# Decode state in half batches through four buffers, and decode key scores with the transposes one step ahead

## The reference

```
def ssd_recurrent(xs, dt, a, bm, cm, h0):            # state update, one step
    h = h * exp(dt * a) + outer(x * dt, b)           # h: 8 x 32 heads x 64 x 128, f32: 1 MB a row
    y = einsum(c, h)                                 # contraction over the 128 states
    return y, h                                      # the new h is an output

def indexer_scores(iq, ik, iw):                      # 8 heads, dimension 64
    dots = relu(einsum('bthd,bsd->bths', iq, ik))    # ik: 4096 cached keys per row, in pages of 128
    return einsum('bths,bth->bts', dots, iw * IDX_SCALE)
```

## Time and profile before

| | us |
|---|---|
| runs of the kernel before | 5871.83, 5881.72, 5880.62 |
| their median | 5880.62 |
| the profiled execution | 5866.49 |
| its span | 5864.7 |
| mix stage with the decode work, layer 0 | 759 to 1112 of the span |
| the same, layer 1 | 3185 to 3545 |

### The profile page before, as it was taken

The page is one execution under the profiler, slowest core; times in us unless marked ns, Lnnn a source line. Parts: engine busy times, 40 slices in busy tenths (PEclk is TensorE's granted clock), DMA queues, the critical chain, the costliest instruction groups (busy, mean ns, idle before and its releaser), DMA issues. The chain is left out here.

```text
span 5864.7 us, 54435 instructions
## 1 busy us (share of the span) xinstructions
PE 4418.7 (75%) x17752; PEld 2782.1 (47%) x17752; DVE 3518.7 (60%) x7869; ACT 1258.5 (21%) x3195; POOL 2478.8 (42%) x2215
## 2 busy tenths in 40 slices
PE   7948356777977798579778676968777677766988
PEld 5338245545444486253344565553334644642333
DVE  4061766596567632876676848966767467374334
ACT  2041132112133201120332311121232112111111
POOL 0000134334543322446565322456655345366776
PEclk9968567788988899889889888988888888888999
DMA  4316388667865585689889955689888977998999
GB/s 136 115 62 221 103 300 309 232 210 247 306 235 190 160 278 168 224 292 378 299 300 328 331 196 195 208 291 346 316 285 301 323 262 263 319 337 339 409 409 383
DMA packets 650608, 1555.20 MB, mean 265 GB/s; under 512 B 61416, under 2 KB 322120, under 8 KB 643816
## 3 DMA queue, kind: packets, MB, share of 16 engines
q0 software_dynamic: 307200, 1115.82, 53.1%
q1 hardware_dynamic: 330168, 401.65, 20.7%
q10 hardware_dynamic: 12960, 34.26, 1.5%
HBM read 1505.63 MB, written 45.93 MB: 265 GB/s over the span
## 5 line engine op out<-in xcount | busy, mean ns | idle before, releaser
L2749 PE MATMUL duo<-vring,diag 128*128 128x512 f32 (+1 forms) x3036 | 1549.3, 660 | 376.8 <-DMA vring<-in_peer_v,eidx 207.2
L2619 POOL DMA_INDIRECT uring<-in_peer_u,eidx x1024 | 1191.7, 1164 | 1373.0 <-DVE uring L2657 1034.5
L2702 POOL DMA_INDIRECT vring<-in_peer_v,eidx x1024 | 1122.2, 1096 | 1362.6 <-PE duo L2749 717.7
L2657 DVE SCALAR_TENSOR_TENSOR uring<-uring,xr 128x1024 f32<-128x1024 f32 x904 | 1091.8, 1221 | 259.2 <-DMA uring<-in_peer_u,eidx 221.9
L2749 PEld LDWEIGHTS duo<-vring,diag 128*128 128x128 f32 (+1 forms) x3036 | 601.8, 208 | 1160.0 <-issue 1010.2
L711 PE MATMUL duo<-wx,xT 128*128 128x512 f32 (+3 forms) x1440 | 605.7, 579 | 30.3 <-PEq L154 30.3
L2730 ACT ACTIVATE diag<-ident,wt 128x128 f32<-128x128 f32 x743 | 281.5, 397 | 823.2 <-PE duo L2749 708.3
L711 PEld LDWEIGHTS duo<-wx,xT 128*128 128x128 f32 (+1 forms) x1440 | 240.8, 179 | 382.5 <-issue 379.7
L2782 DVE SCALAR_TENSOR_TENSOR x_tok<-vring,wt,x_tok 128x1024 f32<-128x1024 f32 x281 | 365.0, 1299 | 65.4 <-DMA vring<-in_peer_v,eidx 39.3
L555 PE MATMUL duo<-xT,wx 128*128 128x264 f32 (+1 forms) x1536 | 356.7, 396 | 20.7 <-ACT newcols L578 17.8
L555 PEld LDWEIGHTS duo<-xT,wx 128*128 128x128 f32 x1536 | 302.0, 198 | 76.5 <-issue 25.1
(11 more groups left out here) (466 smaller groups left out, 5220.1 us busy)
## 6 DMA issues: line engine op xcount, KB each, us to landing
wx<-in_w_in SPq DMA_DIRECT2D x32, 2048.0 KB, 9.4
wx<-in_w_in SPq DMA_DIRECT2D x48, 1024.0 KB, 8.3
wm<-in_w_in SPq DMA_DIRECT2D x48, 1024.0 KB, 11.2
wm<-in_w_branch_a SPq DMA_DIRECT2D x48, 1024.0 KB, 10.6
wq<-in_peer_wq SPq DMA_DIRECT2D x48, 1024.0 KB, 9.7
wm<-in_w_branch_b SPq DMA_DIRECT2D x24, 1024.0 KB, 5.5
wm<-in_w_out SPq DMA_DIRECT2D x24, 1024.0 KB, 7.1
tokm<-tout ACTq DMA_DIRECT2D x64, 256.0 KB
```

The costliest lines, as they stand in the source:

```text
L2619: pool.indirect_dma_start(out=E.rings.urows[K % E.ur], out_offset=None, in_=table, in_offset=bass.IndirectOffsetOnAxis(ap=E.tiles[q][3][:, ...
L2657: dve.scalar_tensor_tensor(row, row, 1.0, xr, ALU.mult, ALU.mult, accum_out=G.pre[:, q % 2, j:j + 1]).then_inc(G.dotted, 1)
L2702: pool.indirect_dma_start(out=E.rings.vrows[K % E.vr], out_offset=None, in_=table, in_offset=bass.IndirectOffsetOnAxis(ap=E.tiles[q][3][:, ...
L2749: mm = pe.matmul(G.bank[6 + c][0:m, :], G.diag[:, R % DR, 0:m], E.rings.vrows[K % E.vr][:, c * BANK:(c + 1) * BANK], start=first, stop=las ...
```

## The change

It has three edits and one table.

State in half batches: `s_h` becomes four buffers of half a row (512 KB) in place of two of a whole one. Load, update and store go by halves i = 2b + hf, and buffer i % 4 is loaded again once half i is reduced and stored.

Outer halves: ACT's two halves of the outer product get places of their own, at b - 0.1 and b + 0.1 rows, where both stood at b + 0.1.

Scores one step ahead: transposes and copies of step e + 1 stand ahead of the dots, relu and reductions of step e, on TensorE, ACT and VectorE. The key gathers move one step earlier on GpSimd.

The table: ssm has 80 units instead of 130, scores 55 instead of 80, the mix stage covers 165 units instead of 240, and job S has 405 in all.

```diff
         self.gss, self.grs = self.sb("gss", [P, 1]), self.sb("grs", [P, 1])
-        self.h, self.u = self.sb("h", [P, 2, CPP, NST]), self.sb("u", [P, CPP, NST])
+        self.h, self.u = self.sb("h", [P, STATE_RING, CPP // 2, NST]), self.sb("u", [P, CPP, NST])
...
-KEYS_STEP, KEYS_RING, KV_RING = 16, 4, 4
+KEYS_STEP, KEYS_RING, KV_RING, STATE_RING = 16, 4, 4, 4
...
 HOT_ROWS = 4 * TOPK_S // PK
-SAMPLE_PARTS = (("ssm", 0.0, 130.0), ("qkv", 130.0, 30.0), ("scores", 160.0, 80.0), ("topk", 240.0, 130.0), ("attend", 378.0, 102.0))
-SAMPLE_TIME = 480.0
+SAMPLE_PARTS = (("ssm", 0.0, 80.0), ("qkv", 80.0, 30.0), ("scores", 110.0, 55.0), ("topk", 165.0, 130.0), ("attend", 303.0, 102.0))
+SAMPLE_TIME = 405.0
...
+def state_half(state, i):
...
+    half = CPP // 2 * NST
+    return state[i // 2].rearrange("h p n -> (h p n)").rearrange("(q x) -> q x", q=P)[:, i % 2 * half:(i % 2 + 1) * half]
...
     G, sem, at, n = J.G, J.sem, span(0), DECB
-    state = [G.state_ssm[J.l, b].rearrange("h p n -> (h p n)").rearrange("(q x) -> q x", q=P) for b in range(n)]
...
+    def load(i):
+        r = i % STATE_RING
+        sp.dma_start(J.h[:, r].rearrange("p c n -> p (c n)"), state_half(G.state_ssm[J.l], i)).then_inc(sem(f"hin{r}"), 16)
...
     sp.dma_start(J.dsk2[:], G.dsk[0:n, :]).then_inc(sem("skip"), 16)
-    for b in range(2):
-        sp.dma_start(J.h[:, b].rearrange("p c n -> p (c n)"), state[b]).then_inc(sem(f"hin{b}"), 16)
+    for i in range(STATE_RING):
+        load(i)
...
     for b in range(n):
+        for hf in range(2):
+            i = 2 * b + hf
+            if i + STATE_RING < 2 * n:
+                yield at(0.2 + 0.65 * (b + 0.8 + 0.2 * hf) / n)
+                sp.wait_ge(sem("reduced"), i + 1)
+                sp.wait_ge(sem(f"hout{i % STATE_RING}"), 16 * (i // STATE_RING + 1))
+                load(i + STATE_RING)
...
         sp.dma_start(J.ytf[CPP * b:CPP * (b + 1), :], J.yq[:, b, :]).then_inc(sem("yin"), 16)
-        if b + 2 < n:
-            sp.wait_ge(sem(f"hout{b % 2}"), 16 * (b // 2 + 1))
-            sp.dma_start(J.h[:, b % 2].rearrange("p c n -> p (c n)"), state[b + 2]).then_inc(sem(f"hin{b % 2}"), 16)
...
     act.activation(J.ztf[:], J.ztf[:], ACT.Silu).then_inc(sem("zs"), 1)
+    yield at(0.2)
+    act.wait_ge(sem("xdq"), 16 * n)
     for b in range(n):
-        yield at(0.2 + 0.65 * (b + 0.1) / n)
-        if b == 0:
-            act.wait_ge(sem("xdq"), 16 * n)
-        act.wait_ge(sem("bcast"), b + 1)
         for hf in range(2):
+            yield at(0.2 + 0.65 * max(0.0, b - 0.1 + 0.2 * hf) / n)
+            act.wait_ge(sem("bcast"), b + 1)
...
             last.then_inc(sem("outer"), 1)
-        yield at(0.2 + 0.65 * (b + 0.6) / n)
-        act.wait_ge(sem("stepped"), 2 * (b + 1))
-        act.dma_start(G.ssm_sample[J.l, b].rearrange("h p n -> (h p n)").rearrange("(q x) -> q x", q=P),
-                      J.h[:, b % 2].rearrange("p c n -> p (c n)")).then_inc(sem(f"hout{b % 2}"), 16)
+        for hf in range(2):
+            i = 2 * b + hf
+            r = i % STATE_RING
+            yield at(0.2 + 0.65 * (b + 0.4 + 0.15 * hf) / n)
+            act.wait_ge(sem("stepped"), i + 1)
+            act.dma_start(state_half(G.ssm_sample[J.l], i), J.h[:, r].rearrange("p c n -> p (c n)")).then_inc(sem(f"hout{r}"), 16)
...
     act.activation(J.grs[:], J.grs[:], ACT.Sqrt).then_inc(sem("groot"), 1)
-    act.wait_ge(sem("hout0"), 16 * n // 2)
-    act.wait_ge(sem("hout1"), 16 * n // 2)
+    for r in range(STATE_RING):
+        act.wait_ge(sem(f"hout{r}"), 16 * 2 * n // STATE_RING)
...
     for b in range(n):
-        hb = J.h[:, b % 2]
...
         for hf in range(2):
-            c = slice(half * hf, half * (hf + 1))
+            c, i = slice(half * hf, half * (hf + 1)), 2 * b + hf
+            hb = J.h[:, i % STATE_RING]
             yield at(0.2 + 0.65 * (b + 0.2 + 0.15 * hf) / n)
-            dve.wait_ge(sem("outer"), 2 * b + hf + 1)
-            if hf == 0:
-                dve.wait_ge(sem(f"hin{b % 2}"), 16 * (b // 2 + 1))
-            dve.scalar_tensor_tensor(hb[:, c], hb[:, c], J.eaq[:, b:b + 1], J.u[:, c], ALU.mult, ALU.add).then_inc(sem("stepped"), 1)
+            dve.wait_ge(sem("outer"), i + 1)
+            dve.wait_ge(sem(f"hin{i % STATE_RING}"), 16 * (i // STATE_RING + 1))
+            dve.scalar_tensor_tensor(hb, hb, J.eaq[:, b:b + 1], J.u[:, c], ALU.mult, ALU.add).then_inc(sem("stepped"), 1)
...
             dve.wait_ge(sem("stepped"), 2 * b + hf + 1)
-            own(dve.tensor_tensor(J.u[:, c], hb[:, c], cb, ALU.mult))
+            own(dve.tensor_tensor(J.u[:, c], J.h[:, (2 * b + hf) % STATE_RING], cb, ALU.mult))
...
         if e >= KEYS_RING:
-            yield at(0.1 + 0.88 * (e - KEYS_RING + 1) / (2 * NE))
+            yield at(0.1 + 0.88 * (e - KEYS_RING) / (2 * NE))
...
         dve.tensor_copy(J.skT[:, e % 2, BANK:], G.bank[4][:]).then_inc(sem("kT_d"), 1)
+    yield at(0.1 + 0.88 * 0.2 / (2 * NE))
+    copy(0)
     for e in range(2 * NE):
-        yield at(0.1 + 0.88 * (e + 0.2) / (2 * NE))
-        copy(e)
         yield at(0.1 + 0.88 * (e + 0.7) / (2 * NE))
+        if e + 1 < 2 * NE:
+            copy(e + 1)
...
     J.enter(act, 2)
-    for e in range(2 * NE):
-        yield at(0.1 + 0.88 * (e + 0.2) / (2 * NE))
...
+    def copy(e):
...
         act.activation(J.skT[:, e % 2, 0:BANK], G.bank[3][:], ACT.Copy).then_inc(sem("kT_a"), 1)
+    yield at(0.1 + 0.88 * 0.2 / (2 * NE))
+    copy(0)
+    for e in range(2 * NE):
         yield at(0.1 + 0.88 * (e + 0.6) / (2 * NE))
+        if e + 1 < 2 * NE:
+            copy(e + 1)
...
     J.enter(pe, 2)
-    for e in range(2 * NE):
-        yield at(0.1 + 0.88 * e / (2 * NE))
...
+    def turn(e):
...
                 tr.then_inc(sem("kturned"), 1)
+    yield at(0.1)
+    turn(0)
+    for e in range(2 * NE):
         yield at(0.1 + 0.88 * (e + 0.4) / (2 * NE))
+        if e + 1 < 2 * NE:
+            turn(e + 1)
...
 ORDER_SAMPLE = BACK + FRONT
-PLAN_SAMPLE = {"mix": 240, "norm2": 4, "pscore": 74, "route": 56, "norm1": 4, "xbc": 32, "tokproj": 70}
-PLAN_SAMPLE_SPLIT = {"mix_b": 240, "norm2_b": 4, "pscore_b": 50, "route_b": 80, "norm1": 4, "xbc": 32, "tokproj": 70}
+PLAN_SAMPLE = {"mix": 165, "norm2": 4, "pscore": 74, "route": 56, "norm1": 4, "xbc": 32, "tokproj": 70}
+PLAN_SAMPLE_SPLIT = {"mix_b": 165, "norm2_b": 4, "pscore_b": 50, "route_b": 80, "norm1": 4, "xbc": 32, "tokproj": 70}
...
```

## The result

| | before | changed kernel |
|---|---|---|
| median of the runs, us | 5876.64 (4 runs) | 5797.09 (4 runs, 5792.99 to 5802.14) |
| ratio, 95% interval | | 0.9865 [0.9848, 0.9882] |
| profiled execution: span, us | 5864.7 | 5792.5 |

The change takes 80 us off, 1.35%.

What follows compares the result with a forecast made beforehand. No engine bounds the whole; in the scores TensorE and VectorE wait for each other, and DMA and VectorE fill the loop. Scores -38, clock -6, loop -10, qkv +10: -44 us, 5822 profiled, 5837 as median; range 5798 to 5872.

Steps and rivals of the forecast that it cites:

- Waits of the scores: Key scores: TensorE's waits before the dots go when transposes run one step ahead; -19 us in each layer.
- Clock: Key scores: dots and transposes return partly to full TensorE clock; -4 us in layer 0, -2 in layer 1.
- State loop: State loop, per layer: less other work -6, 4 KB rows +4, fewer VectorE waits for state loads -3; sum -5 us.
- the term of moved work: State loop: 10.5% of the other 22.3 MB of DMA traffic leaves the loop; -6 us per layer.
- Half transfers: State loop: half batches cut rows from 8 to 4 KB and slow state transfers; +4 us per layer, bounds 0 to +7.
- Prelude and tail: Stretches before and after the state loop: chains of small transfers that fewer instructions beside them don't shorten; 0 us.
- qkv: Stretch before the key scores: takes 0.057 more of the stage's other work; +6 us in layer 0, +4 in layer 1.
- ACT by halves: State loop: outer products earlier in ACT's queue park it longer, taken in by TensorE's idle time; 0 us, bounds 0 to +20.
- B: Rival, chance 0.16: all 16 us of clock return, qkv +0, prelude and tail -14, loop 6 more; -84 us, 5797.
- C: Rival, chance 0.20: in the scores TensorE waits for VectorE's copies before the transposes instead, qkv +14; -15 us, 5866.
- D: Rival, chance 0.06: state halves arrive late in the saturated state loop, +48 us; in all +22 us, 5903.
- E: Rival, chance 0.08: mix stages are held elsewhere, the scores' gains fall to the stage's other chains; no change, 5880.

Runs made afterwards that it cites:

- fill: Kernel before with 8 extra identity transposes per scores step, placed where TensorE waits before the dots; ratio 0.9990 [0.9978, 1.0003].
- table_only: Kernel before with the new table alone (ssm 80, scores 55, mix stage 165 units); ratio 1.0019 [1.0008, 1.0029].
- no_table: Changed kernel with the old table (ssm 130, scores 80, mix stage 240 units); ratio to the kernel before 0.9884 [0.9868, 0.9901].
- state_only: Kernel before with the state in four half buffers and the outer halves placed apart, scores and table as before; ratio 1.0013 [0.9996, 1.003].

## Why the prediction was wrong

*Waits of the scores (-19 and -19).* Right in cause, and near in size. TensorE's idle time fell by 22.2 and 20.8 us, 5 us more than forecast; of it the forecast's leftover of 3 us shows as 5.1 and 1.8 us of waits for VectorE's copy.

*Clock (-4 and -2, bounds -10.2 and -5.9).* This term failed. TensorE's busy time fell by 14.4 and 16.3 us, 31 instead of 6, and that is 25 of the 36 us by which the forecast gain of 44 was short of the 80. Added up by line, 12.7 and 14.7 us of it are faster records, still beyond both bounds. I had priced full clock on two lines alone, dots and transposes, and left out the other lines that run between them, though the earlier trace rows gave the clock for the whole stretch: 0.83 over 96 us of busy time and 0.87 over 114. The two lines kept to their bounds, with 6.9 and 5.0 us. The others, put at nothing, gave 5.8 and 9.7 (L2226 alone 2.1 and 5.2). I then took less than half of a bound that was too small, with the reason that slow sets also follow other idle time. The fill run speaks against that discount: filling the waits before the dots, with the useful work in its old order, already brought 7 and 10 us. The Trainium skill (TensorE: Matmul & The Clock Gate, "Loop structure matters more than you think") puts it so that whether matmuls stay warm is decided by the loop nest. The trace of layer 1 agrees: with the same matmuls and fewer waits between them its clock went from 0.87 to 0.97.

*State loop (-5 and -5).* Layer 0 -3.3, layer 1 -9.3, so 13 instead of 10. By the loops of table_only and no_table the table accounts for most of it, as the term of moved work (-6) had it. The -3 for state waits isn't seen: VectorE's waits for state loads, 9.4 and 6.5 us before, were 9.3 and 5.3 with the ring alone, whose loops stayed at 104 us; in the changed kernel they were 7.1 and 2.3.

*Half transfers (+4 in the loop).* This was put too high. The store queue ran at 406 GB/s with 4 KB rows against 417; at these rates a layer's 16.8 MB of state would cost 41.4 us instead of 40.3, an estimate of +1. The 381 GB/s behind the +4 were those of the expert gathers, another kind of transfer. The Trainium skill's rule of 1 MiB or more per DMA (DMA: Bandwidth & Descriptors, "Measured (HBM→SBUF, 128 partitions, SWDGE, issued from GpSimd)") shows no larger price here: loops of 104 us in state_only as before. The reason I gave, other transfers in flight, fits; it wasn't tested.

*Prelude and tail (0).* -0.9 and -2.3, and -2.3 and -4.8: they shrink a little.

*qkv (+6 and +4).* +6.7 and +11.2: layer 1 was under-priced by 7, and its 11.2 us pass the 10 that the prediction had named as a sign of being wrong. What held qkv there wasn't looked into.

*ACT by halves (0).* No run shows it apart.

Loop, prelude, tail and qkv together gave +0.2 and -5.2; forecast 0. So the sum by terms is -43.0 waits, -30.7 busy time of TensorE, -5.0 other stretches, +6.9 outside the stages: -71.8 of the 72.2 us of span. The medians differ by 7 us more than the spans, which is within what the runs of one kernel spread (5871.83 to 5881.72).

*The rivals.* B forecast 5797, the measured time, but in part by luck, since its errors cancel: its clock gain of 16 us was little more than half of the real one, its prelude and tail (-14) gave 10, its qkv (0) was wrong by 18. C's mechanism exists, at 7 us. D's did not come: 8 waits for state loads, 9.4 us in all, where it asked for 14 late halves at 4 us. (D's own sum adds 8 us for 4 KB rows where its text says 14; with 14 it would be 5909, which changes nothing here.) E's did not come either: both stages gave up 79 us, and the span kept 72 of them. The low end of the range was B's middle, so half of B lay outside, and with the clock bounded too tightly nothing stretched the range further. Of the signs named in advance, the waits before the dots are nearly gone, the stretches took 96 and 107 us (forecast 106 and 127), VectorE's wait for the relu fell from 34.0 to 10.5 us in layer 0, the clock was 0.89 and 0.97, and the loops took 100.5 and 95.4.

## What to carry to other kernels

When waits cut a matmul stream into pieces, price the clock on every line of the stretch, as its busy time times what the clock lacks of 1, and not on the lines that wait. Here this estimate would have been 99.3 x 0.17 + 113.1 x 0.13 = 32 us, and 27 came back, beside 43 of the waits themselves. A handful of useless matmuls in the waits tells in one run whether the clock is at stake and gives a lower figure for it (17 of the 27 here), and the same matmuls in the changed kernel tell whether TensorE has become the bound. In this ring over three engines, running one step ahead took the waits away; moving the consumer later in the queue gave less than half. The likely reason, argued and not tested alone, is that each engine's copy for the next step stands ahead of its wait for this one.

## What the runs showed of the hardware

TensorE's granted clock in a stretch with unchanged useful work went from 0.87 to 0.93 by adding 17 us of transposes to 113 us of matmuls, and the whole kernel took no longer (0.9990 [0.9978, 1.0003]). The same 8 transposes per step made the changed kernel 26 us slower by the medians.

The length of a record follows the clock. In the scores of the kernel before, medians at 1.2 and 2.4 GHz were 421 and 275 ns for 128x64, 634 and 379 for 128x256, and 1061 and 592 for 128x512; 128x256 records of one group started 427 and 216 ns apart.

State transfers of 512 KB in rows of 4 KB ran beside full DMA queues (0.98) nearly as fast as those of 1 MB in rows of 8 KB: 406 against 417 GB/s in the store queue, and the loops' lengths were 104 us with both.
